# A block of gated mixers and experts: w_mod as whole rows, a plain first gate slab, and the norm's transposes inside w_b

## The reference

```
mod = silu(c) @ w_mod + b_mod                  # w_mod 1024 x 6144; six rows: sh1, sc1, g1, sh2, sc2, g2
h   = layer_norm(x) * (1 + sc1) + sh1
a_val, a_gate, (u, v), g_a, g_b = split(h @ w_in + b_in)        # w_in 1024 x 6144
ya  = causal_depthwise_conv(a_val * sigmoid(a_gate))            # 31 taps
ya  = silu(layer_norm(ya)) @ w_a + b_a
yb  = (gelu(u) * (w_s masked, mixed over tokens of layer_norm(gelu(v)) + b_s)) @ w_b + b_b
m   = sigmoid(g_a) * ya + sigmoid(g_b) * yb
x   = layer_norm(alpha * x + g1 * (m @ w_out + b_out))
```

## Time and profile before

| | |
|---|---|
| three runs | 2102.17, 2104.33, 2105.6 us; median 2104.33 |
| profiled execution | 2110.98 us, span 2109.2 us |
| busy, share of the span | TensorE 93%, VectorE 43%, ScalarE 22%, GpSimd 3% |
| mean granted clock of TensorE | 0.976 |
| moved | 581.37 MB, mean 276 GB/s |
| the stages | up to about 360 us the front, experts to about 1350, then the second block |

### The profile page before, as it was taken

How to read it: one execution, slowest core, us unless ns; L and a number is a source line. 1 busy time by engine, 2 the same in 40 slices (tenths; PEclk the granted TensorE clock), 3 DMA queues, 4 the chain that set the end, 5 groups by cost and what they waited for, 6 DMA issues and landing times. The chain is left out here.

```text
span 2109.2 us, 27417 instructions
## 1 busy us (share of the span) xinstructions
PE 1956.5 (93%) x10917; PEld 1228.5 (58%) x10918; DVE 908.0 (43%) x1446; ACT 472.0 (22%) x565; POOL 72.0 (3%) x130
## 2 busy tenths in 40 slices
PE   4999898999999899999999999979999988999998
PEld 2859775433333333333333333358987987878986
DVE  3699644211111111111111121167556787876554
ACT  1223102000000000100000000024543643334542
POOL 2000002000000000000000000010000010020000
PEclk8999997999999999999999999999999989999999
DMA  9785834959999999899999995936555620055552
GB/s 359 246 310 169 292 135 168 413 214 422 422 422 422 422 422 422 343 422 422 422 422 422 383 386 220 364 120 205 181 196 166 198 96 1 1 172 163 190 190 80
DMA packets 143604, 581.37 MB, mean 276 GB/s; under 512 B 10520, under 2 KB 12552, under 8 KB 94281
## 3 DMA queue, kind: packets, MB, share of 16 engines
q1 hardware_dynamic: 136384, 564.43, 68.7%
q0 software_dynamic: 3040, 11.02, 1.7%
q10 hardware_dynamic: 4105, 4.86, 0.7%
HBM read 579.23 MB, written 1.05 MB: 275 GB/s over the span
## 5 line engine op out<-in xcount | busy, mean ns | idle before, releaser
L2482 DVE TENSOR_SCALAR area<-bank 128x512 f32<-128x512 f32 x36 | 24.9, 692 | 723.3 <-PE bank L1214 723.3
L1214 PE MATMUL bank<-ring,area 128*64 128x512 f32 x1280 | 292.4, 603 | 18.9 <-DMA ring<-in_w_gu 18.3
L944 PE MATMUL bank<-area_r,ring_r 128*128 128x256 f32 x992 | 282.6, 285 | 9.3 <-DVE area_r L2203 7.1
L946 PE MATMUL bank<-area_r,ring_r 128*128 128x256 f32 x992 | 281.6, 284 | 0.0
L947 PE MATMUL bank<-area_r,ring_r 128*128 128x256 f32 x992 | 281.5, 284 | 0.0
L296 DVE TENSOR_TENSOR ring_r<-ring,ring_r 128x2048 fp32r<-128x2048 f32 x90 | 205.8, 2291 | 151.0 <-ACT ring_r L293 149.3
L1252 PE MATMUL bank<-ring,area 128*64 128x512 f32 x1152 | 259.3, 597 | 7.7 <-DMA ring<-in_w_dn 6.4
L293 ACT ACTIVATE ring_r<-ring 128x2048 fp32r<-128x2048 f32 x92 | 175.6, 1912 | 180.1 <-PE bank L947 152.4
L1214 PEld LDWEIGHTS bank<-ring,area 128*64 128x64 f32 x1280 | 90.8, 138 | 203.6 <-issue 146.5
L944 PEld LDWEIGHTS bank<-area_r,ring_r 128*128 128x128 f32 x992 | 191.3, 193 | 12.1 <-DVE area_r L2203 7.3
L946 PEld LDWEIGHTS bank<-area_r,ring_r 128*128 128x128 f32 x992 | 191.4, 193 | 0.0
(11 more groups left out here) (348 smaller groups left out, 2245.6 us busy)
## 6 DMA issues: line engine op xcount, KB each, us to landing
ring<-in_w_gu SPq DMA_DIRECT2D x160, 1024.0 KB, 20.7
ring<-in_w_dn SPq DMA_DIRECT2D x128, 1024.0 KB, 20.7
area<-in_w_gu SPq DMA_DIRECT2D x96, 1024.0 KB, 23.3
ring<-in_mlp_w SPq DMA_DIRECT2D x64, 1024.0 KB, 5.4
ring<-in_w_in SPq DMA_DIRECT2D x24, 1024.0 KB, 6.0
ring<-in_gdn_w_in SPq DMA_DIRECT2D x16, 1024.0 KB, 5.5
area<-in_w_mod SPq DMA_DIRECT2D x12, 1024.0 KB, 8.6
ring<-in_w_mod SPq DMA_DIRECT2D x8, 1024.0 KB, 17.1
```

The lines of the kernel that those rows point to most:

```text
L944: ins = mm(out_, a_[0], b_[0], start=start, stop=False)
L946: mm(out_, a_[0], b_[1], start=False, stop=False)
L1214: ins = mm(bk[hf * BLK:(hf + 1) * BLK, :], x(kt), block_u[:, c:c + BANK], start=False, stop=kt == ND - 1)
L2482: step(v.tensor_scalar(g_min, banks[5][:, :], LIMIT, None, ALU.min), w[2])
```

## The change

1. *w_mod in whole rows.* A unit is now 128 rows x 2048 columns (8 KB a row). TensorE waits for one unit at a time and releases each after its four products.
2. *The first gate slab plain.* a_gate_0 is computed by `feature_major` from plain hT; its units are no longer split, so 16 splits remain and all their positions move by two. ScalarE and VectorE write plain hT in turn (banks 0 and 2, banks 1 and 3); ScalarE copies the high part from it afterwards, and a_gate_1 is the first to wait for the parts.
3. *Small inputs later.* w_s, b_s, w_router and router_bc are issued by SyncE behind a_val_0, and mod2_0 is moved behind them. w_s is transposed on TensorE between a_val_0 and mod2_0, and copied by VectorE after the first half of a_val.
4. *The norm inside w_b.* w_b is computed in four half slabs, with convT after the first and yaT after the third. yaT is given convT's banks. VectorE weighs bank 1 after the norm, and banks 2 and 3 ahead of the wait for `late_in`.

```diff
-        def fours(w, cs):
-            return [unit(w, kq, c) for c0 in cs for kq in range(2) for c in range(c0, c0 + 4)]
+        def rows_of(w, c0):
+            return [w[P * kt:P * (kt + 1), c0:c0 + 4 * BANK] for kt in range(ND)]
...
-        add("mod1", fours(w_mod, (0,)))
+        add("mod1", rows_of(w_mod, 0))
         add_slab("a_gate_0", w_in, C)
         add_slab("a_gate_1", w_in, C + 1)
+        add_slab("a_val_0", w_in, 0)
         add_mod2(0)
-        add_slab("a_val_0", w_in, 0)
         add_slab("a_val_1", w_in, 1)
...
-        PRE_PARTS = ("a_gate_0", "a_gate_1", "a_val_0", "a_val_1", "u_0", "u_1", "g_a_0", "g_a_1", "g_b_0")
+        PRE_PARTS = ("a_gate_1", "a_val_0", "a_val_1", "u_0", "u_1", "g_a_0", "g_a_1", "g_b_0")
...
-            group(name, n)
+            group(name, n, align=first_group["convT"] % BANKS if name == "yaT" else None)
...
             for n in range(PRE):
                 load(n)
+                if n == first_unit["a_val_0"] + 1:
+                    full(sp, G("mod1T"))
+                    sp.dma_start(ws_raw, ...).then_inc(ws_in, 16)
+                    emptied(sp, G("cols"))
+                    sp.dma_start(b_s_bc..., ...).then_inc(b_s_in, 16)
+                    sp.dma_start(w_router[:, :, :], ...).then_inc(rows_in, 16)
+                    sp.dma_start(router_bc[:, :], ...).then_inc(rows_in, 16)
...
+            def half_slab(name, xT, s, q):
+                n0 = first_unit[name] + 2 * s
+                u = [unit_ready(n0), unit_ready(n0 + 1)]
+                g = G(name, 2 * s + q)
+                claim(pe, g)
+                for m in range(2):
+                    for k in range(ND):
+                        ... (as in feature_major, for one q)
+                fills(ins, g)
+                owed[0] = q == 1
...
-                u = [unit_ready(n0 + j) for j in range(4)]
-                for k in range(UK):
+                for i in range(UK):
+                    kt, s = UK * kq + i, slot_of(n0 + i)
+                    pe.wait_ge(w_full[s], landed_count(n0 + i))
                     for j in range(4):
-                        ins = mm(bank(g)[32 * j:32 * j + 32, :], cond[:, UK * kq + k, :], u[j][:, k, :], ...)
+                        ins = mm(bank(g)[32 * j:32 * j + 32, :], cond[:, kt, :],
+                                 slot_area[s][:, BANK * j:BANK * (j + 1)], start=kt == 0, stop=kt == ND - 1)
                         settle(ins)
-                        if k == UK - 1 and not (kq == 1 and j == 3):
-                            ins.then_inc(w_used, 1)
+                    if kt < ND - 1:
+                        ins.then_inc(w_used, 1)
...
-            feature_major_early("a_gate_0", "a_gate", h_parts, 0, lambda h: pe.wait_ge(h_low, 2 + 2 * h))
-            feature_major_early("a_gate_1", "a_gate", h_parts, 2)
+            feature_major("a_gate_0", "a_gate", hT, 1, x_there=lambda k: emptied(pe, G("hT", k // 2)))
+            feature_major_early("a_gate_1", "a_gate", h_parts, 2, lambda h: pe.wait_ge(h_low, 2 + 2 * h))
             feature_major_early("a_val_0", "a_val", h_parts, 0)
+            pe.wait_ge(ws_in, 16)
+            for q in range(2):
+                transposed(G("wsT", q), [(ws_raw[:, 4 * q + i, :], i * P) for i in range(4)])
             mod2_part(0)
...
-            feature_major("w_b", "w_b", feat(5), 1)
+            half_slab("w_b", feat(5), 0, 0)
             pe.wait_ge(conv_ready, 1)
             to_tokens("convT", feat(3))
-            feature_major("w_b", "w_b", feat(5), 1, first=1, unit0=2)
+            half_slab("w_b", feat(5), 0, 1)
+            half_slab("w_b", feat(5), 1, 0)
             to_features("yaT", tok(8), xn_ready, NT)
+            half_slab("w_b", feat(5), 1, 1)
...
-            for q in range(4):
+            for q in (0, 2):
                 g = G("hT", q)
                 full(act, g)
                 for m in (2 * q, 2 * q + 1):
-                    ins = f(feat_r(1)[:, m, :], bank(g)[...], ACT.Identity, ...)
-                ins.then_inc(h_high, 1)
-            early.below(4)
+                    ins = f(feat(8)[:, m, :], bank(g)[...], ACT.Identity, ...)
+                empties(ins, g)
+            for q in range(4):
+                emptied(act, G("hT", q))
+                f(feat_r(1)[:, 2 * q:2 * q + 2, :], feat(8)[:, 2 * q:2 * q + 2, :], ACT.Copy).then_inc(h_high, 1)
+            early.below(2)
...
-            for q in range(2):
-                weigh("w_b", 7, q)
+            weigh("w_b", 7, 0)
             for q in range(4):
                 emptied(dve, G("convT", q))
             all_stats(tok(8))
             normalise(tok(8), tok(8), xn_ready)
+            weigh("w_b", 7, 1)
...
-            dve.wait_ge(late_in, 64)
             for q in range(2):
                 weigh("w_b", 7, 2 + q)
-                for k in (2 * q, 2 * q + 1):
-                    bias_thirds(k // 2, k % 2)
+            dve.wait_ge(late_in, 64)
+            for k in range(4):
+                bias_thirds(k // 2, k % 2)
```

More of the change, by code:

```diff
@@ L157, in add @@
             stream.extend((name, u) for u in units)
-        mod2_halves = fours(w_mod, (4, 8))
+        mod2_units = rows_of(w_mod, 4 * BANK) + rows_of(w_mod, 8 * BANK)
         def add_slab(name, w, c):
@@ L413, in build @@
             sizes[name] = nxt - g0
-        sizes["gateT"] = 1
+        sizes["gateT"], sizes["convT"] = 1, 4
         for name in names:
@@ L679, in _ @@
                 load(n)
+                if n == first_unit["a_val_0"] + 1:
+                    full(sp, G("mod1T"))
+                    sp.dma_start(ws_raw, A["w_s"][0].rearrange("g i j -> i g j")).then_inc(ws_in, 16)
+                    emptied(sp, G("cols"))
+                    sp.dma_start(b_s_bc.rearrange("p g i -> p (g i)"),
+                                 A["b_s"][0].rearrange("(o g) i -> o (g i)", o=1).to_broadcast([P, D]))\
+                        .then_inc(b_s_in, 16)
+                    sp.dma_start(w_router[:, :, :], A["w_router"][0].rearrange("(k p) e -> p k e", p=P))\
+                        .then_inc(rows_in, 16)
+                    sp.dma_start(router_bc[:, :], A["b_router"][0:1, :].to_broadcast([P, NE])).then_inc(rows_in, 16)
             for n, (e, u) in enumerate(load_order):
@@ L905, in feature_major @@
                                 c = (2 * q + m) * P
+                                if q == 0 and m == 0:
+                                    x_there(k)
                                 ins = mm(bank(g)[:, m * S:(m + 1) * S], u[k // UK][:, k % UK, c:c + P],
@@ L912, in feature_major @@
                     owed[0] = True
+            def half_slab(name, xT, s, q):
[5 more added lines that the diff above has]
+                    for k in range(ND):
+                        c = (2 * q + m) * P
+                        ins = mm(bank(g)[:, m * S:(m + 1) * S], u[k // UK][:, k % UK, c:c + P],
+                                 xT[:, k, :], start=k == 0, stop=k == ND - 1)
+                        settle(ins)
+                        if q == 1 and m == 1 and k == UK - 1:
+                            ins.then_inc(w_used, 1)
+                fills(ins, g)
+                owed[0] = q == 1
             def token_major(name, gname, lhs, n_slab, bias=None, first=0):
@@ L1767, in modulation_row @@
                 full(act, g)
+                full(act, G("wsT", 1))
                 empties(f(mod_row[:, r, :], bank(g)[:, :], ACT.Copy), g)
+            early.below(3)
+            pairs("a_gate", gate_a, (0, 1))
             early.below(5)
[L1771 to L1772 removed]
             pairs("a_gate", gate_a, (2, 3))
[L1774 removed]
+            early.below(6)
             modulation_row(0)
             gelu_v(0)
[L1777 removed]
+            early.below(8)
             gelu_v(1)
             modulation_row(1)
+            early.below(11)
+            pairs("u", gelu_u, (0, 1))
             early.below(13)
[L1781 removed]
+            pairs("u", gelu_u, (2, 3))
             early.below(15)
[L1783 to L1784 removed]
             pairs("g_a", sigmoid_a, (0, 1))
[L1786 removed]
+            early.below(16)
             pairs("g_a", sigmoid_a, (2, 3))
@@ L2164, in _ @@
             empties(v.tensor_copy(cols[:, 0:c0], bank(g)[:, 0:c0]), g)
[L2165 to L2171, removed]
             dve.wait_ge(x_in, 16)
@@ L2190, in _ @@
             early = EarlySplitter(dve, "low")
-            early.below(1)
-            for q in range(4):
+            for q in (1, 3):
                 g = G("hT", q)
-                dve.wait_ge(h_high, q + 1)
                 full(dve, g)
@@ L2201, in _ @@
                 empties(ins, g)
-                emptied(dve, g)
+            for q in range(4):
+                dve.wait_ge(h_high, q + 1)
                 v.tensor_tensor(feat_r(2)[:, 2 * q:2 * q + 2, :], feat(8)[:, 2 * q:2 * q + 2, :],
                                 feat_r(1)[:, 2 * q:2 * q + 2, :], ALU.subtract).then_inc(h_low, 1)
-            early.below(8)
+            early.below(6)
             dve.wait_ge(consts, 1)
@@ L2248, in _ @@
```

(11 more changed lines are left out.)

25 lines of the change are left out of this document (9 added, 16 removed).

## The result

The changed kernel ran in 2091.01 us (median of six runs, 2087.49 to 2096.77), the kernel before in 2104.97 (2102.17 to 2111.28): a ratio of 0.9922 [0.9902, 0.9942]. It is faster, by 14 us and not by 26.5, and 2091.01 lies outside the range of 2072 to 2086. The profiled execution took 2092.7 us with a span of 2091.0, against 2110.98 and 2109.2.

A forecast was written before the change was run, and what follows sets the result against it. Expert transfers were taken to be released by TensorE's progress, so an earlier expert start counts whole at the end. 12.4 - 0.95 + 4.6 + 0 + 10.5 = 26.5 us off 2104.33 gave 2077.8 us, range 2072 to 2086.

The forecast's parts named there:

- Part 1: The front, to a_val_0's end: first gate slab starts 14.8 us earlier, itself takes 2.4 us more, 12.4 us gained.
- the 2.3 left in: First gate slab: about 2.3 us lost at the lower clock level, assumed to stay.
- A: The end of a_val_0, forecast to move from 83.57 to 71.2 us, 12.4 us earlier.
- Rival 2: The front gives half, through worse-shared transfers or ineffective row size, plus clock: slab at 34 to 35, 2081 to 2085; chance 0.12.
- both low bounds: Front: moving small inputs saves only 3.1 us, whole rows of w_mod nothing; first gate slab at 33.5.
- Part 2: Between a_val_0's end and w_b: w_s transposes lose 0.95 us, mod2_1's vanished wait and steady clock gain 4.6 us.
- The slack: Before convT: VectorE's convolution ends 1.1 us before TensorE asks for it, so cost 0, bounds 0 and 3.8.
- rival 1: VectorE becomes the bound before convT or a split: 2079 to 2084 us; chance 0.2.
- Part 3: The convolution's norm inside w_b: waits between w_b and w_a covered by half slabs, 10.5 us gained, low bound 7.
- the experts pass it on: Expert stage: TensorE's progress releases the transfers, so every microsecond of earlier start counts as one at the end.
- rival 3: The experts absorb the saving because transfers are the true bound, started elsewhere: 2104 us; chance 0.03.
- Rival 4: Slower: small inputs on SyncE's in-order queue hold up mod2_0 and later slabs: 2110 us; chance 0.02.

The follow-up runs named there:

- e4: Changed kernel, but SyncE issues each later unit of w_mod only when the unit two before it has landed; packed vectors there at 16.26 us.
- e1: Changed kernel with the twelve loads of packed vectors issued by SyncE ahead of w_mod instead of by ScalarE; 2084.12 us, ratio 0.9900 to the kernel before.
- e8: Repetition of e1, the changed kernel with packed vectors issued by SyncE ahead of w_mod; ratio 0.9876 to the kernel before.
- e3: Kernel before with w_mod in whole rows and nothing else of the change; median 2118.21 us, slower by 0.4%.

## Why the prediction was wrong

**The step that failed** is in Part 1: "From 26.5: TensorE uses each unit as it lands, so the last costs 0.6 us, not 5.3", and with it the first gate slab at 32.0. w_mod itself came about as forecast ("complete at 33.0 - 6.5 = 26.5 us"): its last byte was moved at 26.3 us. But the packed vectors, and so `cond`, were taken to come as early as before, and the sum has no term for them. They landed at 25.43 instead of 13.04, so the whole modulation, 6.26 + 3.64 us of matmuls, was still to do when w_mod was there, and the slab started at 42.88. The sign that the prediction named for this part, w_mod landing after 29, did not even come. The accounting of transfers was by bytes, as if the 11.30 MB of the earlier trace rows came in the order in which they are wanted. It asked when the largest transfer is complete and never when the smallest is, though the chain starts there: packed vectors, cols, cond, modulation. Their packets are counted in the trace of the changed kernel. From 2 to 25 us ScalarE's queue, which carries x and them, sent 903, 1.30 MB:

```profile
DMA packets 1981, 9.22 MB, mean 401 GB/s; under 512 B 263, under 2 KB 759, under 8 KB 1015
...
q1 hardware_dynamic: 1078, 7.91, 85.0%
q10 hardware_dynamic: 903, 1.30, 15.5%
```

By turns, 903 packets of w_mod go in the meantime, 7.4 MB at 8 KB; with 1.30 MB at 401 GB/s that is 21.7 us, and with the 2 us before the first byte and the 1.1 after the last some 24.8, measured 25.43. With 2 KB rows the same 903 turns are 1.85 MB, and at the 357 GB/s of that stretch 8.8 us, so some 11.9, measured 13.04. Both are estimates with exactly equal turns. Over the whole stretch q1 sent 1078 packets, not 903: it was ahead before 4 us (56 to 23) and again from 20 to 24 us (228 to 130), and no run shows why the turns were not equal at that end. The rows to see this were in the trace of before: from 12 to 16 us its q1 and q10 sent as many packets as each other. The term came out as 4.0 us (46.83 to 42.88) where 14.8 was forecast. The slab's price was right in the undisturbed case (14.05 us in e4, 13.9 forecast), the clock took some 1.8 us of it, less than the 2.3 left in, and A moved 2.1 us instead of 12.4.

The Trainium skill ("DMA: Bandwidth & Descriptors", Queues, rings and completion order) has each transfer engine go round between the queues that hold work, a whole packet at a time, a packet being typically 9 to 17 descriptors. The trace agrees on the turns (217 to 215, and 577 to 578). Whether one or several of the packets recorded go in a turn would give the same counts, and no run here tells.

**Rival 2** said that the transfers might share worse than the bytes say. That was the direction, at a price of 2 to 3 us instead of 11. It too was made from bandwidth, and reached up to 2085.

**With that one cause taken away the forecast nearly holds.** In e1 and e8 the first gate slab starts at 33.6 and 33.5 (forecast 32.0), waiting for its own weights as forecast; A is at 72.14 in e1 (71.2), and w_a's end comes 26.0 to 26.1 us earlier (26.5). The last unit of w_mod lands at 28.0 to 28.2, not at 26.5. In e1 SyncE issues w_mod only from 5.45 us on, behind the twelve small loads; from 5 to 6 us, with 450 of 465 packets under 2 KB, 231 GB/s were moved, and from 6.5 to 7.5 us only 20 packets went. In whole time the ratios are 0.9900 [0.9884, 0.9917] and 0.9876 [0.9853, 0.9898], which is 21 and 26 us.

**Two workings in Part 1 are off and change nothing.** With both low bounds (3.1 us for the small inputs, nothing for the rows) w_mod is complete at 29.9 and the slab starts at 35.3, not at 33.5. And 82.9 us for 288 matmuls of one line are 0.288 us each, not 0.120; the 0.120 is right, but it is the distance between the starts of neighbouring matmuls, which overlap.

**Part 2 was right.** The convolution ends at 210.53 + 11.16 = 221.69, A + 140.2 (forecast A + 141.2), and TensorE asks for it at 223.76, A + 142.3 (A + 142.3). The slack was 2.1 us, not 1.1, and rival 1 did not come. mod2_1 does not wait and the clock stays, so the 4.6 us came, less the 0.95 of the w_s transposes.

**Part 3 was right**, with 11.0 us in the changed kernel and 11.3 alone (10.5; the clock gave all of its 1.8 and not 1.5). yaT starts right behind three half slabs, silu lies under the fourth.

**That the experts pass it on was right.** The first expert matmul is 16.2 us earlier, w_a's end 16.7, so rival 3 is out for this saving: the ratio of 0.9922 is 16.4 us. Rival 4, a hold of SyncE by the small inputs, did not come: b_router's issue took 1.96 us there, not 7.03, and TensorE has no wait behind it in the changed kernel.

## What to carry to other kernels

Where two DMA queues run side by side, count packets and not bytes: a queue of small rows moves as many packets as its neighbour while both hold work, and making the neighbour's rows four times as large made the small transfers nearly twice as late here (13.0 to 25.4 us). Before enlarging rows, ask which small load starts the chain, and issue it ahead of them on the same queue, as e1 does (8.4 us). And read the equal counts in the trace of the kernel that you have; they are there before the change is made.

## What the runs showed of the hardware

- Two queues took turns by packet at 8 KB to 512 B and less (217 to 215) as at 2 KB to the same (577 to 578), but not from 8 to 12 us of e4 (130 to 629), where SyncE held only two units in flight.
- SyncE's issue of the eight units of w_mod, 1 MB each, took 3.92 us with 8 KB rows:

```profile
0.81 3.92 SPq L670 DMA_DIRECT2D ring<-in_w_mod  x8
```

  and 18.05 us with 2 KB rows in the kernel before. The issue of a small transfer of ScalarE, w_router's 128 KB, took 15.16 us in e3 and 2.38 in the kernel before. Before it on its queue stood the same loads in both, but in e3 they moved more slowly; that this held the issue is argued and not shown.
- While small packets went nearly alone, less was moved: 231 GB/s in e1 from 5 to 6 us, where 450 of 465 packets were under 2 KB, against 424 GB/s from 8 to 12 us, where nearly all were of 8 KB. From 4 to 8 us as a whole, which takes in 0.49 MB of x in 4 KB rows and the near standstill from 6.5 to 7.5 us:

```profile
DMA packets 794, 1.10 MB, mean 275 GB/s; under 512 B 143, under 2 KB 631, under 8 KB 750
```
